# Routing from the unnormed rows: RMSNorm's weights folded into the router's weights, its reciprocal root applied to the logits, and the rows turned by halves

## The reference

```python
h = h + jnp.concatenate([conv_out, attn_out], axis=-1) @ w_o
hn = h * lax.rsqrt(jnp.mean(h * h, -1, keepdims=True) + EPS) * norm_ffn
logits = hn @ w_router + b_router          # 1024 x 32
top_vals, top_idx = lax.top_k(logits, 4)
gates = softmax(top_vals)
# each chosen expert: clamped SwiGLU of hn, weighted by its gate, summed onto h
```

## Time and profile before

| | us |
|---|---|
| median of 3 runs | 2291.48 (2290.32 to 2299.23) |
| the profiled execution's own time | 2284.88 |
| its span | 2283.0 |
| TensorE matmul busy | 2123.9 (93%) |
| TensorE weight load busy | 1923.6 (84%) |
| VectorE, ScalarE, GpSimd busy | 730.0, 404.3, 558.1 |

### The profile page before, as it was taken

The page is one execution under the profiler, slowest core; times in us unless marked ns, Lnnn a source line. Parts: engine busy times, 40 slices in busy tenths (PEclk is TensorE's granted clock), DMA queues, the critical chain, the costliest instruction groups (busy, mean ns, idle before and its releaser), DMA issues.

```text
span 2283.0 us, 42195 instructions
## 1 busy us (share of the span) xinstructions
PE 2123.9 (93%) x15622; PEld 1923.6 (84%) x15623; DVE 730.0 (32%) x1930; ACT 404.3 (18%) x1018; POOL 558.1 (24%) x637
## 2 busy tenths in 40 slices
PE   6999997899984899999999999999999999999992
PEld 5888885455544899999999999999999999999992
DVE  0222222333323233433233332333333333343331
ACT  1221212323211111111111111111111111111110
POOL 1122221010022223223322332222232322323321
PEclk9999998999986999999999999999999999999996
DMA  7000004212104889999998999999999989999997
GB/s 271 10 18 9 9 1 147 56 28 56 29 19 143 263 261 323 315 291 290 296 294 273 310 296 289 299 289 288 271 302 311 315 262 273 315 316 314 301 289 85
DMA packets 305781, 486.70 MB, mean 213 GB/s; under 512 B 106786, under 2 KB 128162, under 8 KB 305698
## 3 DMA queue, kind: packets, MB, share of 16 engines
q1 hardware_dynamic: 249394, 441.14, 59.2%
q0 software_dynamic: 33120, 44.91, 9.4%
q10 hardware_dynamic: 23232, 0.18, 0.6%
HBM read 454.81 MB, written 35.84 MB: 215 GB/s over the span
## 4 chain that ended last, share of the span: by engine, by line
PE 88%; DVE 3%; issue 3%; SPq 1%; ACT 1%; DMA 1%; POOL 1%; ACTq 0%; DVEq 0%; POOLq 0%
PE psum L975 41%; PE psum L991 22%; PE psum L798 7%; PE psum L940 5%; PE psum L811 2%; PE psum L889 1%; PE psum L846 1%; PE psum L814 1%; PE psum L888 1%; PE psum L923 1%; PE psum L852 1%; PE psum L906 1%; PE psum L952 1%; DMA area<-in_x 1%; DVE area L1289 1%
## 5 line engine op out<-in xcount | busy, mean ns | idle before, releaser
L975 PE MATMUL psum<-area 128*128 128x128 f32 (+2 forms) x8192 | 994.4, 284 | 40.9 <-issue 23.1
L975 PEld LDWEIGHTS psum<-area 128*128 128x128 f32 x8192 | 985.7, 192 | 46.4 <-issue 46.3
L991 PE MATMUL psum<-area 128*128 128x128 f32 (+2 forms) x4096 | 502.8, 284 | 1.6
L991 PEld LDWEIGHTS psum<-area 128*128 128x128 f32 x4096 | 491.2, 191 | 10.7 <-DVE area L1289 9.9
L1270 DVE TENSOR_SCALAR area<-psum,area 128x160 f32<-128x160 f32 x256 | 86.5, 379 | 628.5 <-PE psum L975 628.5
L575 POOL DMA_INDIRECT sum_rows<-area x165 | 261.8, 1587 | 67.3 <-issue 40.2
L737 ACT ACTIVATE area<-area 128x320 f32<-128x320 f32 x128 | 60.2, 470 | 754.2 <-DVE area L1270 754.2
L798 PEld LDWEIGHTS psum<-area 128*128 128x128 f32 x1536 | 176.2, 194 | 3.8 <-issue 3.3
L798 PE MATMUL psum<-area 128*128 128x128 f32 x1536 | 177.6, 277 | 0.0
L565 POOL DMA_INDIRECT area<-normed_rows,area x165 | 160.5, 972 | 62.1 <-issue 61.8
L560 POOL TENSOR_TENSOR area<-area 128x5 uint32<-128x5 uint32 x33 | 6.2, 189 | 644.4 <-DVE area L1255 607.1
(11 more groups left out here) (187 smaller groups left out, 1273.4 us busy)
## 6 DMA issues: line engine op xcount, KB each, us to landing
area<-in_w_gate_up SPq DMA_DIRECT2D x256, 1024.0 KB, 6.3
area<-in_w_down SPq DMA_DIRECT2D x128, 1024.0 KB, 6.9
area<-in_x SPq DMA_DIRECT2D x16, 512.0 KB, 4.0
area<-in_w_in SPq DMA_DIRECT2D x1, 4096.0 KB, 12.9
area<-in_w_o SPq DMA_DIRECT2D x1, 4096.0 KB, 13.7
sum_rows<-area SPq DMA_DIRECT2D x32, 128.0 KB, 2.7
normed_rows<-area SPq DMA_DIRECT2D x8, 512.0 KB, 2.8
out<-sum_rows SPq DMA_DIRECT2D x4, 1024.0 KB, 13.8
```

Source lines behind the costliest of these rows:

```text
L975: ins = mm(dst, w_gu[piece][:, k, c * P:(c + 1) * P], xT[:, PART * s + k, 0:width], start=(s == 0 and k == 0 and c % 2 == 0), stop=(s == 1 ...
L991: ins = mm(bank[4 + d // 3][:, (d % 3) * SLOTS:(d % 3) * SLOTS + width], w_dn[q][:, kk, d * P:(d + 1) * P], actT[:, 2 * q + kk, 0:width], ...
```

## The change

- HT is split. HA i turns the first 512 columns of the row (bank 4, copied out by ACT), HB i the other 512 (bank 5, copied out by DVE). Both read h_sb, the row before its norm. HA i-2 stands at head 0 ahead of WO 2(i-2)+1, HB i-2 at head 2 where HT stood. At the end: OT 7, HB 6, RT 6, WO 14, RK 6, WO 15, HA 7, HB 7, RT 7, RK 7.
- norm_ffn is also loaded as g_ffn (8 values on each partition, by single elements) and multiplied into w_r once, by DVE, ahead of the step S 8.
- The router's bias is spread over all partitions by its DMA and no longer waited for by TensorE's bias turn; the matmul of L953 is gone. DVE's logit step becomes one instruction, bank 7 times the row's reciprocal root plus the bias.
- ACT squares each half of the row after its own half of WO: after the even half also an Identity that adds eps, after the odd half the root with that value as its bias. In the last tile a root whose result nobody reads stands after the even half.
- hf is still made and stored for the experts. SP's load of the next x row now also waits for HB i.

```diff
         if h == 0 and i > 1:
+            steps.append(("HA", i - 2))
             steps.append(("WO", 2 * (i - 2) + 1))
         if h == 2 and i > 1:
-            steps.append(("HT", i - 2))
+            steps.append(("HB", i - 2))
...
-    return steps + [("OT", e), ("HT", e - 1), ("RT", e - 1), ("WO", 2 * e), ("RK", e - 1),
-                    ("WO", 2 * e + 1), ("HT", e), ("RT", e), ("RK", e)]
+    return steps + [("OT", e), ("HB", e - 1), ("RT", e - 1), ("WO", 2 * e), ("RK", e - 1),
+                    ("WO", 2 * e + 1), ("HA", e), ("HB", e), ("RT", e), ("RK", e)]
...
-            sp.dma_start(br_row[0:1, :], I["b_router"]).then_inc(bias_in, 16)
+            sp.dma_start(br_row, I["b_router"].to_broadcast([P, E])).then_inc(row_in, 16)
...
+            sp.dma_start(g_ffn, I["norm_ffn"][0].rearrange("(k p) -> p k", p=P), allow_slow_non_contiguous=True).then_inc(row_in, 16)
...
                 if i + 2 < NT:
+                    sp.wait_ge(turn_b, use_b[("HB", i)])
...
-                if kind == "WO" and n % 2:
-                    i = n // 2
+                if kind == "WO":
+                    i, c = n // 2, n % 2
                     act.wait_ge(h_ready, n + 1)
-                    if i:
-                        act.wait_ge(turn_a, use_a[("HT", i - 1)])
-                        act.wait_ge(turn_b, use_b[("HT", i - 1)])
+                    if i and c == 0:
                         act.wait_ge(hf_out, 16 * i)
-                    A(hf, h_sb[i % 2], ACT.Square, scale=1.0 / D ** 0.5, accum_out=ms_h[:, i:i + 1]).then_inc(h_sq, 1)
-                    act.wait_ge(h_sq, i + 1)
-                    A(sd_h[:, i:i + 1], ms_h[:, i:i + 1], ACT.Sqrt, bias=eps).then_inc(h_std, 1)
+                    cols = slice(c * 512, c * 512 + 512)
+                    A(hf[:, cols], h_sb[i % 2][:, cols], ACT.Square, scale=1.0 / D ** 0.5,
+                      accum_out=(ms_first, ms_h)[c][:, i:i + 1]).then_inc(h_sq, 1)
+                    if c == 0:
+                        act.wait_ge(h_sq, 3 * i + 1)
+                        A(ms_eps[:, i:i + 1], ms_first[:, i:i + 1], ACT.Identity, bias=eps).then_inc(h_sq, 1)
+                        if i == NT - 1:
+                            A(sd_h[:, i:i + 1], ms_first[:, i:i + 1], ACT.Sqrt, bias=eps)
+                    else:
+                        act.wait_ge(h_sq, 3 * i + 3)
+                        A(sd_h[:, i:i + 1], ms_h[:, i:i + 1], ACT.Sqrt, bias=ms_eps[:, i:i + 1]).then_inc(h_std, 1)
...
-            pe.wait_ge(bias_in, 16 * 3)
+            pe.wait_ge(bias_in, 16 * 2)
...
+                if kind == "HB":
+                    pe.wait_ge(h_ready, 2 * n + 2)
+                    if use_b[(kind, n)] > 1:
+                        pe.wait_ge(turn_b_read, use_b[(kind, n)] - 1)
+                    for k in range(KD // 2):
+                        ins = tr(bank[5][:, k * P:(k + 1) * P], h_sb[n % 2][:, 512 + k * P:512 + (k + 1) * P], ident)
+                    ins.then_inc(turn_b, 1)
...
+                    pe.wait_ge(turn_a_read, use_a[("HA", n)])
                     for k in range(KD):
-                        mm(bank[7][:, 0:E], hfT[:, k, :], w_r[:, k, :], start=(k == 0), stop=False)
-                    mm(bank[7][:, 0:E], ones[0:1, :], br_row[0:1, :], start=False, stop=True).then_inc(rt_done, 1)
+                        if k == KD // 2:
+                            pe.wait_ge(turn_b_read, use_b[("HB", n)])
+                        ins = mm(bank[7][:, 0:E], hfT[:, k, :], w_r[:, k, :], start=(k == 0), stop=(k == KD - 1))
+                    ins.then_inc(rt_done, 1)
...
+                if kind == "S" and n == 8:
+                    dve.wait_ge(w_r_in, 16)
+                    dve.wait_ge(row_in, 16 * 3)
+                    V.tensor_tensor(w_r, w_r, last(g_ffn, E), ALU.mult).then_inc(w_r_ready, 1)
...
-                    V.tensor_copy(lg, bank[7][:, 0:E]).then_inc(lg_read, 1)
+                    V.scalar_tensor_tensor(lg, bank[7][:, 0:E], rs_h[:, n:n + 1], br_row, ALU.mult, ALU.add).then_inc(lg_read, 1)
```

More of the change, by code:

```diff
@@ L199, in build @@
         stat = sb("stat", [P, 40])
-        attn_stat = sb("attn_stat", [P, 128])
+        attn_stat = sb("attn_stat", [P, 144])
         gsum = sb("gsum", [P, 2])
@@ L271, in build @@
         bias_rows = take(2 * FF + D)
-        lg, top8, idx8, idxf, br_row = take(E), take(8), take(8), take(NT, 8), take(E)
+        lg, top8, idx8, idxf, br_row, g_ffn = take(E), take(8), take(8), take(NT, 8), take(E), take(KD)
         e4, entry_bits = take(TOPK), take(NT * TOPK * 2).bitcast(U32)
@@ L326, in build @@
         pool_chain, dve_chain = sem("pool_chain"), sem("dve_chain")
+        w_r_ready = sem("w_r_ready")
         w_o_in, w_r_in, row_in, bias_in = sem("w_o_in"), sem("w_r_in"), sem("row_in"), sem("bias_in")
@@ L356, in build @@
             kind, n = st
-            if kind in ("TP", "OT", "HT"):
+            if kind in ("TP", "OT", "HA"):
                 use_a[st] = len(use_a) + 1
-            if kind == "HT" or (kind == "TP" and n // HEADS >= 4):
+            if kind == "HB" or (kind == "TP" and n // HEADS >= 4):
                 use_b[st] = len(use_b) + 1
@@ L678, in _ @@
             nm, = (attn_stat[:, 120:128],)
+            ms_first, ms_eps = attn_stat[:, 128:136], attn_stat[:, 136:144]
             n_evac = [0, 0]
@@ L704, in _ @@
                     A(attnT, bank[4].rearrange("p (k n) -> p k n", k=HEADS), ACT.Copy).then_inc(turn_a_read, 1)
-                if kind == "HT":
+                if kind == "HA":
                     act.wait_ge(turn_a, use_a[(kind, n)])
@@ L901, in _ @@
                         src = [o_sb[:, k * P:(k + 1) * P] for k in range(HEADS)]
-                    if kind == "HT":
-                        pe.wait_ge(hf_ready, n + 1)
-                        src = [hf[:, k * P:(k + 1) * P] for k in range(KD)]
+                    if kind == "HA":
+                        pe.wait_ge(h_ready, 2 * n + 1)
+                        src = [h_sb[n % 2][:, k * P:(k + 1) * P] for k in range(KD // 2)]
                     for k, s in enumerate(src[0:4]):
@@ L942, in _ @@
                 if kind == "RT":
-                    pe.wait_ge(turn_a_read, use_a[("HT", n)])
-                    pe.wait_ge(turn_b_read, use_b[("HT", n)])
-                    pe.wait_ge(w_r_in, 16)
+                    pe.wait_ge(w_r_ready, 1)
                     pe.wait_ge(h_ready, RT_H[n])
@@ L1171, in _ @@
                     if c:
-                        if i == 0:
-                            dve.wait_ge(row_in, 16)
                         dve.wait_ge(h_std, i + 1)
```

## The result

| | before | after |
|---|---|---|
| median of 6 runs each on one chip, us | 2291.92 (2290.32 to 2299.23) | 2263.72 (2256.14 to 2266.83) |
| ratio, with its 95% interval | | 0.9867 (0.9847 to 0.9888) |
| the profiled execution's own time, us | 2284.88 | 2265.45 |
| its span, us | 2283.0 | 2263.6 |
| TensorE matmul busy, us | 2123.9 | 2121.4 |

Faster, as forecast, but by more: 1.33% of 2291.5 is 30.5 us where 17.2 were forecast. So TensorE's busy time of these two, 2.5 us apart, can't be compared either.

The account below looks back on a forecast made before the run. Heads bound by TensorE with short stalls, then a serial chain over the engines; the experts' stage unchanged. Gains 20.8 less losses 3.6 give 17.2 us net: 2291.5 to 2274.3 us, range 2263 to 2284.

Parts of the forecast that it names:

- the end: Last rows, from OT 7 to the experts: earlier router, no bias matmul, shorter chain after WO 15; 9.8 us gained.
- parts 1 to 4: Heads: half-row square 2.4 us gained, HT split net 3.5, router 1.7, ACT's new work after even halves 0.5 lost.
- the 0.25 of tile 6: PV's wait behind WO's odd half: at tile 6 the half square saves about 0.25 us, its next wait being close.
- part 4: After WO's even half, ACT's new work delays TP's copy: 0.5 us lost, mostly at tile 1, nothing after tile 2.
- rival A: Heads' stalls refill at the next step, so only the end gains, 10 us: 2281 us; chance 0.14.
- rival C: Clock falls at the starts of WO, 1.6 us per step; slower than before, 2308 at worst; chance 0.04.
- rival B: TensorE keeps full clock through the last rows because gaps are shorter: 5 us more, 2269 us; chance 0.16.
- part 5: Loads on SP's queue: single elements take about 3.3 us, hidden from the x rows; bias turn gains 0.3 us.
- The 0.3 us of the bias turn: Start of stage 2: the bias turn no longer waits for the router's bias load; 0.3 us gained (0 to 0.46).
- Rival D: Identity or Square on ACT lies in another function table, costing 3 to 10 us, about 2281 us; chance 0.05.

Follow-up runs that it names:

- x5: The kernel after with 32 semaphore increments ahead of TensorE's wait for the table, putting the experts' code where it lay before; 2275.11 us, ratio 0.9924.
- x1: The kernel after with 32 NOPs ahead of TensorE's table wait, which never reached the program, so a repeat of after; 2259.21 us, ratio 0.9856.
- x3: The kernel after with HA moved from head 0 to head 2, beside HB, for all tiles; 2262.37 us, ratio 0.9868.
- x4: The kernel after with one square over the whole row after the odd half, no Identity, no early root; 2266.90 us, ratio 0.9890.
- x12: The kernel after with HA beside HB at head 2 for tiles 0 to 5 only, HA 6 ahead of WO 13; 2261.00 us, ratio 0.9872.
- x2: The kernel before with 224 NOPs ahead of TensorE's table wait, which never reached the program, so a repeat of before; 2293.68 us, ratio 1.0002.
- x7: The kernel after with 168 unread identity turns keeping TensorE busy ahead of stage 2 and the experts; 2267.95 us, ratio 0.9883.
- x10: The kernel after with 160 semaphore increments at the start of TensorE's program; 2267.76 us, ratio 0.9894.
- x11: The kernel after with 192 semaphore increments at the start of TensorE's program; 2271.12 us, ratio 0.9902.

## Why the prediction was right or wrong

**The step that failed: "the change adds and takes nothing there", said of the experts' stage.** The experts' work is the same, and their time isn't. Of the 30.5 us, the part with the experts' code held in place (x5) is 0.0076 x 2292.3 = 17.4 us (13.5 to 21.1); the forecast's sum was 17.2. That these agree so closely is partly luck: as the next paragraphs show, the end gave 4 us more than forecast and the heads less, and in x5's profiled execution the end was slow. The other 11 to 13 us (13.1 by the ratios, 11.4 by the medians) are the position: x5's experts take 1512.4 us, those of after, x1, x3, x4 and x12 1498.8 to 1501.6. Some 8 to 10 of them lie in tiles 0 to 2, and the rest, 3.4, in up to 0.3 us for each of the 29 later tiles. The forecast named a change of over 3 us in that stage as what would prove it wrong, and so it did. What one could have seen in the profile of before is the 9.85 us line "issue" in the chain at 771.70, and that the change takes instructions out ahead of it. I had read the chain only as far as the table. Its sign could not have been had from that: the same view gives no rule for which position is a good one.

That this is the fetching of instructions is inferred. For it: the standstills have no semaphore behind them, they come in the first passes through the experts' code (later there is only one of about 1 us, at 2146 in before), they follow the position in all runs, and the program's instruction queue moved 23 packets of 16 KB before and 22 after, two of them (starting at 773.7 and 777.2) within the 9.85 us and one (at 766.0) within the 5.66. Not explained by it: the up to 0.3 us of each later tile, whose code had been run before.

**The heads (parts 1 to 4, -6.7 us to WO 13).** Mechanisms right: OT's copy stands at Exp's end in head 2, the logit step is 0.25, no L953, the half square 0.63, no load at Identity. First scores to WO 13 fell from 269.4 to 267.1 (before to x1, short start) and from 280.9 to 275.9 (x2 to after, long start), less than forecast. In the first pair the clock hides a part: it was at half for 18.5 us of that stretch before and for 25.2 in x1. In the second it was the same, 47.4 and 47.6 us. With half of these times taken off the differences are -5.7 and -5.0.

Place by place, before against x1: the stretch at head 2 became shorter by 0.90, 0.90, 1.17, 1.19, 1.20 and 1.22 us, 6.6 in all as forecast. HA took 0.44 in each of its seven places, as forecast. A router step with its WO became 0.28 shorter, as forecast. The waits of PV behind the odd halves fell by 0.42, 0.42, 0.43 and 0.34, and not by the 0.25 of tile 6: 1.6 for 2.0. The term that was mis-sized is part 4: behind the even halves 0.43 and 1.22 us were lost, 1.65 for 0.5. These add up to -5.2.

So rival A (stalls refilled) falls. The half clock of rival C (the clock falls where WO starts) was there, at one to four of the WO steps and not at eleven: steps of 8.6 to 8.8 us after the first pair number two before and four in x1, three in x2 and four in after. But its reason, the turns of HA ahead of WO, does not fit: HA stands ahead of the odd WO steps, and these took 7.03 us up to WO 13 in every trace; the falls that met a WO met an even one, behind the router. Whether the new order causes more of them is open: x3 had one, x12 two, x5 one, so they vary from execution to execution.

**The end (-10.2 us from WO 13 to the experts' first matmul).** Measured 84.2 to 69.7 (before, after) and 84.5 to 70.0 (x2, x1): -14.5. After WO 15 it is 12.1 to 5.9, 6.2 for the 6.4 forecast. The excess of 4 us lies ahead of it and is rival B: WO 14 at 7.11 and not 8.75, the router of tile 6 at 1.80 and not at half clock. The half-clock stretch there was 652 to 670 before and 657 to 661 after. It did not come every time: in x5 and x7, whose steps there are those of after, the stretch lasted 14 us (652.7 to 666.3 in x5) and WO 13 to the first expert matmul took 74.6 and 74.1; in after, x1, x10 and x11 it took 69.7 to 70.0. The forecast gave B 5 us and a chance of 0.16, though the shorter gaps that it rests on were the forecast's own; it should have been in the main case in part.

**The even half (part 4).** After WO 0 the copy for TP ran at 402.38, and PV at 402.80, 1.4 us behind the residual add's end as forecast. Of the later even halves the chain shows one, which the forecast had at nothing: after WO 12 the copy starts at 643.75, 0.99 behind the add's end at 642.76, and TensorE stands idle 1.47 us ahead of PV, where it was 0.25 before. Eight key blocks do not cover it, since PV needs this copy first.

**The loads (part 5).** SP's queue of after, start and us:

```profile
364.83 0.76 SPq L409 DMA_DIRECT2D area<-in_w_router  x1
365.64 10.56 SPq L410 DMA_DIRECT2D area<-in_norm_ffn  x1
376.24 3.91 SPq L411 DMA_DIRECT2D area<-in_norm_ffn  x1
380.20 0.91 SPq L413 DMA_DIRECT2D area<-in_x  x2
```

L410 is the load of single elements, L411 the row that the earlier trace rows has as L408. The x rows are issued 5.3 us later than in the earlier trace rows, and are first needed at 400.7: hidden, as said. From SP's first issue to theirs it is 17.2 us, for 11.2 before: the single elements cost the queue 6.0 us, for the 3.3 estimated. The 0.3 us of the bias turn did not come: from SP's first issue to the first scores it is 7.7 us before and in after, since b_down, now the last one waited for, lands 3.4 us after its own issue.

**Rival D** (Identity in another table) is refuted: at 643.55 it runs in 0.29 us right behind Square, with no load. The Trainium skill (ScalarE: Activation LUTs, Table sets) says that identity is in every set; here the trace agrees.

**The scale.** The forecast took the change off the median of before, 6.6 us above the profiled execution. That was right, and the traces give the likely reason: this execution had the short start, and x2, the same kernel with the long one, took 2296.02.

Open: what decides between the short and the long start, and where the short falls come; which positions of the code are good; and whether HA's place costs in clock what it gains.

## What to carry to other kernels

A change that adds or removes instructions ahead of a long loop also moves the loop's code; here that was worth 11 to 13 us of 30. To know what an edit itself is worth, put in as many instructions that do nothing as it removed, where the engine waits anyway (make sure that they are in the program, unlike the empty ones of x1, and few: 32 and 96 left no standstill, 224 did), and look for "issue" lines in the chain of waits of the loop's first passes. Before two profiled executions are subtracted, compare their half-clock stretches; a sum that comes out right can hold terms that missed both ways.

## What the runs showed of the hardware that was not expected

- 96 instructions without work, ahead of the experts, made the kernel before faster by 0.5% (0.9949, 0.9925 to 0.9973); 32 made the kernel after slower by 11 to 13 us.
- A row of semaphore increments on TensorE is dear where it is long: standstills of 14.7, 19.7 and 24.8 us for 160, 192 and 224 at the start of the program, 18.7 for 224 ahead of the experts, none to be seen for 32 or 96 there.
- At the start of stage 2 the clock was at half for 21 or for 38 us, in the same kernel. In after it stayed at half from 370.8 to 394.5, with TensorE busy 23.0 of these 23.7 us. Short falls of 3 to 4 us came later, each at some 1.7 us. Identity turns held the clock at full while they ran, and it fell to half behind them (x7).
- On SP's queue the issue behind the loads of w_o (4096 KB) and w_r took 8.8 us before and 10.6 after.
